# Attention core of a hybrid encoder: the mask of the prompt rows is summed with the bias on POOL, and the last remainder of the core is made ahead of the last output tiles

## The reference

```python
score = jnp.where(adm, score, -jnp.inf)
_, idx = lax.top_k(score, n_sel)             # the keys that a query may look at
logits = jnp.einsum('qgrd,qkgd->qgrk', qg, kg).astype(jnp.float32) * HEAD_DIM ** -0.5
bias = rel_table[rel_bucket(k_pos[idx] - qp[:, None])]
logits = logits + bias...                    # one bias per head and distance
logits = jnp.where(ok[:, None, None, :], logits, NEG_INF)
p = jax.nn.softmax(logits, axis=-1)
```

## Time and profile before

| what | value |
|---|---|
| median of 3 runs | 1788.16 us (1787.98 to 1788.22) |
| the profiled execution's own time | 1787.89 us |
| its span | 1786.1 us |
| PE busy | 1769.6 us, 99% |
| DVE busy | 1066.6 us, 60% |
| ACT busy | 716.3 us, 40% |
| POOL busy | 212.9 us, 12% |
| core of layer 0, core of layer 3 | about 79 to 170 us, about 1390 to 1478 us |

### The profile page before, as it was taken

One profiled execution on the slowest core, in us unless ns is written; L12 is line 12 of the kernel. 1 busy time (PEld: TensorE's weight loads), 2 busy tenths in 40 slices (PEclk: granted clock), 3 DMA queues, 4 the chain that ended last, 5 costly groups with the idle time before them and its releaser, 6 DMA issues.

```text
span 1786.1 us, 27858 instructions
## 1 busy us (share of the span) xinstructions
PE 1769.6 (99%) x10034; PEld 1733.9 (97%) x10034; DVE 1066.6 (60%) x1856; ACT 716.3 (40%) x1139; POOL 212.9 (12%) x258
## 2 busy tenths in 40 slices
PE   9999999999999999999999999999999999999998
PEld 8988999999999999999999999999999889999998
DVE  7876855544487755554476655554457867555533
ACT  5365433333378433333232333333323664333331
POOL 5000300001115400001100200000140004000011
PEclk9999999999999999999999999999999999999999
DMA  8311333333333433334433333333455113433441
GB/s 304 125 36 60 119 120 126 118 119 129 119 117 106 135 129 117 120 115 141 130 118 129 119 118 117 117 119 128 136 171 180 60 48 102 133 129 118 130 138 62
DMA packets 63844, 216.96 MB, mean 121 GB/s; under 512 B 7153, under 2 KB 8769, under 8 KB 63521
## 3 DMA queue, kind: packets, MB, share of 16 engines
q1 hardware_dynamic: 59520, 202.25, 34.3%
q0 software_dynamic: 3280, 12.12, 2.3%
q10 hardware_dynamic: 976, 1.70, 0.3%
HBM read 212.38 MB, written 3.66 MB: 121 GB/s over the span
## 4 chain that ended last, share of the span: by engine, by line
PE 92%; DVE 4%; ACT 3%; issue 1%; DMA 0%; DVEq 0%; ACTq 0%
PE bank L703 27%; PE bank L702 27%; PE bank L701 27%; PE bank L901 1%; PE bank L878 1%; PE bank L857 1%; PE bank L859 1%; PE bank L858 1%; DVE w_lo L1310 1%; PE bank L920 1%; ACT w_hi L1028 1%; PE bank L884 1%; PE bank L927 0%; PE bank L804 0%; PE bank L928 0%
## 5 line engine op out<-in xcount | busy, mean ns | idle before, releaser
L701 PE MATMUL bank<-a_hi,w_hi 128*128 128x400 f32 (+2 forms) x1936 | 673.4, 348 | 1.6 <-DVE w_lo L1310 1.1
L1310 DVE TENSOR_TENSOR w_lo<-raw,w_hi 128x1024 fp32r<-128x1024 f32 x382 | 490.3, 1288 | 306.7 <-ACT w_hi L1028 305.1
L702 PE MATMUL bank<-a_lo,w_hi 128*128 128x400 f32 (+2 forms) x1936 | 666.0, 344 | 0.0
L703 PE MATMUL bank<-a_hi,w_lo 128*128 128x400 f32 (+2 forms) x1936 | 665.3, 344 | 0.0
L1028 ACT ACTIVATE w_hi<-raw 128x1024 fp32r<-128x1024 f32 x382 | 399.9, 1052 | 345.6 <-PE bank L703 338.0
L701 PEld LDWEIGHTS bank<-a_hi,w_hi 128*128 128x128 f32 (+1 forms) x1936 | 362.5, 187 | 6.0 <-issue 1.9
L703 PEld LDWEIGHTS bank<-a_hi,w_lo 128*128 128x128 f32 (+1 forms) x1936 | 364.9, 188 | 0.7
L702 PEld LDWEIGHTS bank<-a_lo,w_hi 128*128 128x128 f32 (+1 forms) x1936 | 362.7, 187 | 2.6
L703 PE MATMUL bank<-h_hi,w_lo 128*128 128x400 f32 (+1 forms) x704 | 240.8, 342 | 0.0
L702 PE MATMUL bank<-h_lo,w_hi 128*128 128x400 f32 (+1 forms) x704 | 240.1, 341 | 0.0
L701 PE MATMUL bank<-h_hi,w_hi 128*128 128x400 f32 (+1 forms) x704 | 239.2, 340 | 0.0
(11 more groups left out here) (255 smaller groups left out, 1754.4 us busy)
## 6 DMA issues: line engine op xcount, KB each, us to landing
raw<-in_w_all SPq DMA_DIRECT2D x382, 512.0 KB, 3.4
bias_p<-rel_scratch POOLq DMA_DIRECT2D x2, 2176.0 KB, 10.6
k_s<-in_ck_t POOLq DMA_DIRECT2D x4, 512.0 KB, 8.5
v_c<-in_cv POOLq DMA_DIRECT2D x2, 1024.0 KB, 15.5
ki_s<-in_cki_t POOLq DMA_DIRECT2D x4, 256.0 KB, 5.5
x<-in_x_t SPq DMA_DIRECT2D x2, 400.0 KB, 6.3
x<-in_x_t ACTq DMA_DIRECT2D x2, 400.0 KB, 6.8
out_v_t<-v_f POOLq DMA_DIRECT2D x2, 400.0 KB, 5.1
```

The lines of the kernel that those rows point to most:

```text
L701: pe.matmul(out, wh, hi[:, kc, c0:T], start=(first and n == 0), stop=False)
L702: pe.matmul(out, wh, lo[:, kc, c0:T], start=False, stop=False)
L703: mm = pe.matmul(out, wl, hi[:, kc, c0:T], start=False, stop=(last and n == len(blocks) - 1))
L1310: nc.vector.tensor_tensor(w_lo[:, s, :], raw[:, s, :], w_hi[:, s, :].bitcast(F32), ALU.subtract).then_inc(lo_ready, 1)
```

## The change

The mask product L877 leaves PE for the 64 prompt items. POOL adds the mask to the bias instead, for each prompt item, into one of three buffers `bm`, and DVE reads the sum in the place of the bias. Sample and meta items are as before. Two of the buffers lie over `sq` and `sqsum`, which are not in use in the core; the third has memory of its own. In the last DVE step `low` of the last group comes ahead of the three `half_out`.

```diff
+            def rows_of_core(a):
+
+                pool.wait_ge(in_bias, 96 * (a + 1))
+                pool.wait_ge(vt_done, a + 1)
+                for j, n in enumerate(PROMPT[a]):
+                    _, gp, (t, gi, r) = ITEMS[a][n]
+                    keys = width(ITEMS[a][n])
+                    pool.wait_ge(masks, 3 * a + 1 + t)
+                    if j >= 3:
+                        pool.wait_ge(lg_ready, IB[a] + PROMPT[a][j - 3] + 1)
+                    pool.tensor_tensor(bm[j % 3][:, 0:keys], backwards(bias_p[:, 4 * (2 * gp + gi) + r, 0:keys]), mask[t][:, 0:keys],
+                                       ALU.add).then_inc(biased_ready, 1)
...
                     pool.dma_start(v_t[a], v_f[:]).then_inc(out_sem, 16)
+                    rows_of_core(a)
...
                         t, gi, r = what
-                        pe.wait_ge(masks, 3 * a + 1 + t)
                         pe.wait_ge(evacuated, t0 + 9 + 4 * gp + r + 1)
-                        pe.matmul(ps, ident_b[:], mask[t][:, 0:keys], start=True, stop=False)
-                        mm = pe.matmul(ps, q_t[:, 4 * gp + r, 128 * t:128 * t + 128], kz[:, gi, gp, 0:keys], start=False, stop=True)
+                        mm = pe.matmul(ps, q_t[:, 4 * gp + r, 128 * t:128 * t + 128], kz[:, gi, gp, 0:keys], start=True, stop=True)
...
                     if kind == "prompt":
                         t, gi, r = what
-                        bias = bias_p[:, 4 * (2 * gp + gi) + r, 0:keys]
+                        j = PROMPT[a].index(n)
+                        dve.wait_ge(biased_ready, PB[a] + j + 1)
+                        bias = bm[j % 3][:, 0:keys]
...
+                    if n == N_IT[a] + LAG_LO - 1:
+                        low(len(LAST[a]) - 1)
...
                     for g, e in enumerate(LAST[a]):
-                        if e + LAG_LO == n and OUT[a][g][1]:
+                        if e + LAG_LO == n < N_IT[a] + LAG_LO - 1 and OUT[a][g][1]:
                             low(g)
```

More of the change, by code:

```diff
@@ L130 @@
 GB = [0, len(GROUPS[0])]
+PROMPT = [[n for n, it in enumerate(ITEMS[a]) if it[0] == "prompt"] for a in range(2)]
+PB = [0, len(PROMPT[0])]
 def buffer_of(a, g):
@@ L244, in program @@
         gate_s, up_s, silu_s, hid_s = (sb(n, [128, T]) for n in ("gate_s", "up_s", "silu_s", "hid_s"))
+        rsq = cursor[0]
         sq, sqsum, std, rstd = (sb(n, [128, T]) for n in ("sq", "sqsum", "std", "rstd"))
@@ L271, in program @@
         ident = cst[:, C_ID:C_ID + 128]
+        bm = [at("bm0", [128, NP_TOK], F32, rsq), at("bm1", [128, NP_TOK], F32, rsq + 1088), sb("bm2", [128, NP_TOK])]
         R = Region(rh, hbytes)
@@ L379, in program @@
         lg_done, lg_ready = sem("lg_done"), sem("lg_ready")
-        ex_done, pn_ready = sem("ex_done"), sem("pn_ready")
+        ex_done, pn_ready, biased_ready = sem("ex_done"), sem("pn_ready"), sem("biased_ready")
         tr_done = sem("tr_done")
@@ L1559, in reduced @@
                         t, gi, r = what
-                        bias = bias_p[:, 4 * (2 * gp + gi) + r, 0:keys]
+                        j = PROMPT[a].index(n)
+                        dve.wait_ge(biased_ready, PB[a] + j + 1)
+                        bias = bm[j % 3][:, 0:keys]
                     elif kind == "sample":
-                        bias = bias_s[:, gp, :]
+                        bias = backwards(bias_s[:, gp, :])
                     else:
-                        bias = bias_m[:, gp, :]
-                    nc.vector.tensor_tensor_reduce(lg[n % NL][:, 0:keys], logit_bank(a, n)[:, 0:keys], backwards(bias), -1.0, 3.0e38,
+                        bias = backwards(bias_m[:, gp, :])
+                    nc.vector.tensor_tensor_reduce(lg[n % NL][:, 0:keys], logit_bank(a, n)[:, 0:keys], bias, -1.0, 3.0e38,
                                                    ALU.add, ALU.min, nmx[:, n % 8:n % 8 + 1]).then_inc(lg_ready, 1)
```

## The result

The changed kernel takes 1792.05 us (median of 14 runs, 1791.33 to 1794.03) against 1787.95 us (14 runs) of the kernel before: ratio 1.0023, 95% interval 1.0015 to 1.0031. It is **4.1 us slower**; 1782.5 was forecast, 1779.0 to 1785.8 the range. The profiled execution's span is 1790.9 us. The 14 runs fall in two groups by the mean granted TensorE clock: seven at 0.999 with 1791.33 to 1791.67 us (median 1791.43), seven at 0.998 or 0.997 with 1792.42 to 1794.03.

A forecast was written before the change was run, and what follows sets the result against it. PE was taken to bound the kernel. 7.4 - 2.1 - 2.4 + 2.75 = 5.65 us off the profiled 1787.89 gave 1782.25, and with 0.27 for the median 1782.5 us; range 1779.0 to 1785.8.

The forecast's parts named there:

- What bounds the kernel: Whole span: PE, busy 1769.6 of 1786.1 us, bounds the kernel; a microsecond PE loses is one of the result.
- The removed mask products: PE's queue: 32 products of 144 keys at 0.11 us and 32 of 272 at 0.12, 7.4 us off.
- What DVE keeps: First steps of both cores: DVE has no pause, so about 1.05 us a core of the gain stays there, -2.1 us.
- the other 20 products count in full: Behind item 12 of a core: a group's values give DVE time, so 20 mask products bring their whole price.
- What POOL's work costs DVE: First 12 steps of a core: sums slow `normalise` and splits beside them, 1.2 us a core, -2.4 us.
- 0.05 for each `normalise`: First 12 steps: eleven `normalise` beside sums, each 0 to 0.14 us longer, taken as 0.05 us.
- The splits: First 12 steps: some three splits beside sums, each 0 to 0.6 us longer, taken as 0.2 us.
- Later in the core DVE's idle time covers it: Behind the first 12 steps: DVE's idle time hides contention; without it up to 20 more `normalise` a core would count.
- The end of the cores: In front of the product behind each core: PE's stalls of 1.20 and 1.58 us for `b_lo` vanish, +2.75 us.
- contention eats the mask: Rival, first steps: POOL beside DVE costs 3.3 us a core, 1.45 us are left, 1786.7 us; chance 0.15.
- POOL as the bound: Rival, wide items in a row and second half: sums of 2.6 us lose 13 us, 1795.5 us; chance 0.05.
- `normalise` twice as long through the whole core: Sign on DVE, over the whole core, that the forecast is wrong: `normalise` takes double its time.

## Why the prediction was wrong

With the measured sizes its sum comes out: 1787.95 - 2.9 (end of the cores) - 3.6 (masks) + 10.6 (POOL beside DVE) = 1792.05. 9.6 of the 10.6 are there at full clock; the other 1.0 is clock that PE lost in some of the runs, a cost that the prediction did not have at all.

- **What bounds the kernel:** right. A microsecond that PE waits is one of the result; the 22.7 us that DVE got longer cost only what DVE had no idle time for.
- **The removed mask products, 7.4 us:** the price of one is right where PE sets the pace. In the run without masks items 38, 39 and 40 come 0.09 to 0.11 us earlier each.
- **What DVE keeps, -2.1 us:** too small, -3.8 measured (7.4 - 3.6). Two failures. Item 12 was to come 0.3 us earlier and came 0.02 earlier; the step granted PE a gain in a stretch in which it had itself found DVE without a pause. And "the other 20 products count in full" was never looked at: in the second block of layer 0 items 26 to 36 bring 0.2 us, since DVE is without idle time over part of it. In the kernel before it has none in front of the reductions of items 31 to 33 (timeline of DVE, rows that did not stand ahead of the prediction):

```profile
128.68 0.44 DVE L1566 CUSTOM_DVE_ANT_0 lg<-bank,bias_p 128x272 f32<-128x272 f32 x1
...
130.00 0.44 DVE L1566 CUSTOM_DVE_ANT_0 lg<-bank,bias_p 128x272 f32<-128x272 f32 x1
...
131.95 0.31 DVE L1566 CUSTOM_DVE_ANT_0 lg<-bank,bias_p 128x144 f32<-128x144 f32 x1
```

- **What POOL's work costs DVE, -2.4 us: the step that failed.** Measured 10.6. It took "0.05 for each `normalise`", from the 0.14 us by which the earlier trace rows's one-operand operation exceeded, and argued that a sum is short. The 0.14 was read as a surcharge on DVE's instruction, when that instruction had been held to the end of a copy of only 0.31 us and ended 0.24 behind it. The right reading compares ends: a short instruction beside a longer POOL instruction lasts as long as that. By it `normalise` would be 0.55 to 0.6 us beside a 144 sum, 0.8 to 0.9 beside a 272 sum, 0.3 to 0.5 us each and not 0.05, for eleven of them in the first steps about 4 to 5 us a core; 4.9 was measured up to item 12. The upper end of the range, 3.3 us a core, was made from the same 0.14 and so did not hold it.
- **The splits, 0.2 us each:** nothing in the change, where they stay untouched as `normalise` takes the hit. The prediction read the 1.82 us in the earlier trace rows beside the squares instruction of 176.71, which started 0.8 us later. POOL's instruction in front of that one, which the rows leave out, explains it:

```profile
175.45 1.18 POOL L573 TENSOR_TENSOR sq<-x 128x400 f32<-128x400 f32 x1 [1.33 <-DVE x L1353]
```

It was at work when the split came at 175.89, and ended at 176.63. The split ended 1.08 us after that (177.71), and the squares instruction of 176.71 ended 0.91 us after the split: each waited its turn. So the same rule could have been read in the trace of the kernel before.
- **Later in the core DVE's idle time covers it:** right for the most part (1.5 us lost with the sums in the second block alone).
- **The end of the cores, +2.75 us:** right, 2.9 alone and 2.5 beside the sums (3.0 at full clock).
- **The rivals:** "contention eats the mask" named the mechanism and "each sum starts exactly when `normalise` is due" named the place; it was given 0.15 and a price of 6.6 us. The slower side was given to POOL as the bound, which it never was. What the prediction wrote under Wrong, "`normalise` twice as long through the whole core", is what the profile shows for the items that have a sum beside them (0.53 to 0.90 us for 0.29 to 0.36).

The Trainium skill, "GPSIMD Engine Reference" (section 8), which the prediction weighed, says only that the two engines contend in such cases. The page that prices it was not weighed: "SBUF — State Buffer" (section "Who interferes with whom") says that the shared pair of ports is locked for a whole instruction, that whoever issues first gets it while the other "fully blocks", that DVE's 2-port modes and its two-SBUF-input instructions contend, and that an instruction with one SBUF input outside those modes does not. The runs agree on each: `normalise` held to the end of POOL's instruction, a sum of 0.71 us stretched to 1.52 behind a split, MAX8 and MATCH_REPLACE8 at 0.44 and 0.43 us beside a sum. They add that a `normalise` recorded 0.02 to 0.04 us ahead of the sum lost to it nevertheless (84.78 and 84.82), where its two-operand form won at the same distance (94.55 and 94.58): the recorded starts don't tell who was first when they are that near.

What stays open: no view names the mode of an instruction. The rates bear on it: undisturbed `normalise` costs (362 - 295) / 128 = 0.52 ns a column as TENSOR_SCALAR, and (442 - 313) / 128 = 1.01 ns as TENSOR_TENSOR, so the held form works at twice the rate. When PE loses clock after a wait was not tested either. The two kernels with all 64 sums behind the reduction and the moved `low` lost some in 7 of 14 and 6 of 11 runs, the sums alone in 1 of 5, the kernel before in 3 of 27, the runs without sums in none of 5.

## What to carry to other kernels

When work is moved to POOL, price the DVE instruction that its trigger puts it beside, at POOL's whole duration and not at a share, and then choose the trigger: a wait that lets the sum start one instruction later was worth 9.3 us here. Put such work beside DVE instructions that kept their time beside a sum here (reductions that read PSUM, maximum searches), or where DVE has idle time. Before two medians that differ by less than about 1 us are compared, look at the granted clock of each run. And where two engines set the pace in turn, look for idle time in every stretch before a gain on one of them is counted.

## What the runs showed of the hardware

- A one-operand DVE instruction (TENSOR_SCALAR, f32, SBUF to SBUF) beside a POOL instruction that starts at its side ends 0.08 to 0.10 us behind it with 144 columns, 0.15 to 0.17 with 272 and 0.24 with 416: 0.30 us of 144 columns became 0.40, 0.43, 0.51, 0.56, 0.58 or 0.84 by POOL's length. A POOL copy with one operand does it as well as a sum.
- The same multiplication as TENSOR_TENSOR costs 0.02 us (144 columns) and 0.08 (272) more, and there POOL waited.
- POOL's sum of f32, read backwards, and bf16 takes 0.46 us for 144 columns and 0.71 for 272 undisturbed. That is no more than the squares' 1.04 us for 400 columns gives by share, 0.71 for 272; a reversed copy of 144 columns takes 0.31, as the plain one in the earlier trace rows.
- TensorE's granted clock fell to 0.50 (1.2 GHz) for about 3.4 us in one execution of the change, behind idle stretches of 1.25 and 0.88 us, and stayed at 1.00 behind the same stretches in another kernel.
